# A two-layer hybrid encoder: the first loads in another order, the first two weight chunks by quarters, and GpSimd scaling part of the tokens

## What is computed

```python
def rmsnorm(x, g):
    y = x32 * lax.rsqrt(jnp.mean(x32 * x32, axis=-1, keepdims=True) + EPS)
    return (y * g).astype(x.dtype)

def hybrid_layer(x, c, ...):
    mod = jax.nn.silu(c) @ w_mod + b_mod
    shift, scale, gate = jnp.split(mod, 3, axis=-1)
    h = rmsnorm(x, norm_g) * (1.0 + scale[:, None]) + shift[:, None]
    z = h @ w_in          # 2752 columns, split among three groups of heads
    ...                   # convolution, latent attention, windowed attention
    out = jnp.concatenate([out_conv, out_mla, out_swa], axis=-1) @ w_out
    return x + gate[:, None] * out, states
```

## Time and profile before

| what | value |
|---|---|
| runs | 1207.41, 1207.62, 1209.09 us; median 1207.62 |
| the profiled execution: its own time | 1207.39 us |
| its span, first to last instruction | 1205.6 us, so 1.8 us lie around it |
| TensorE (PE) busy | 96% of the span |
| VectorE (DVE), ScalarE (ACT), GpSimd (POOL) busy | 52%, 36%, 5% |
| TensorE begins with chunk 0 | 41.79 us |
| TensorE begins with chunk 2 | 73.31 us |

### The profile page before, as it was taken

The page is one execution under the profiler, slowest core; times in us unless marked ns, Lnnn a source line. Parts: engine busy times, 40 slices in busy tenths (PEclk is TensorE's granted clock), DMA queues, the critical chain, the costliest instruction groups (busy, mean ns, idle before and its releaser), DMA issues.

```text
span 1205.6 us, 17889 instructions
## 1 busy us (share of the span) xinstructions
PE 1159.5 (96%) x7246; PEld 1039.4 (86%) x7246; DVE 623.6 (52%) x1063; ACT 436.7 (36%) x768; POOL 57.9 (5%) x46
## 2 busy tenths in 40 slices
PE   4699999999999999999999999999999999999996
PEld 3589999999996666789999999999999766769996
DVE  4852333336458866663385233233554886666135
ACT  3442221222246543441265323123223744445122
POOL 1000001000000000002130000100000000000211
PEclk9899999999999999999999999999999999999998
DMA  9621120111123244364131211111102342116003
GB/s 332 244 71 38 35 70 16 41 55 42 55 84 139 99 150 149 105 249 145 47 115 36 74 35 35 51 36 36 57 13 101 110 161 79 45 35 227 1 27 132
DMA packets 71884, 107.72 MB, mean 89 GB/s; under 512 B 3960, under 2 KB 59392, under 8 KB 70528
## 3 DMA queue, kind: packets, MB, share of 16 engines
q1 hardware_dynamic: 71808, 106.68, 26.4%
HBM read 93.91 MB, written 11.70 MB: 88 GB/s over the span
## 4 chain that ended last, share of the span: by engine, by line
PE 86%; DVE 8%; ACT 3%; DMA 1%; issue 1%; SPq 0%; POOLq 0%; DVEq 0%; ACTq 0%
PE psum L900 56%; PE psum L1264 5%; PE psum L1317 5%; PE psum L1296 2%; ACT rot L1462 1%; PE psum L891 1%; PE psum L1254 1%; DVE w_lo L1908 1%; DVE h_lo L1800 1%; PE psum L1331 1%; PE psum L1217 1%; PE psum L1253 1%; PE psum L1313 1%; PE psum L1102 1%; PE psum L1271 1%; PE psum L1274 1%
## 5 line engine op out<-in xcount | busy, mean ns | idle before, releaser
L900 PE MATMUL psum<-h_hi,w_hi 128*128 128x384 f32 x1392 | 473.3, 340 | 14.3 <-DVE h_lo L1858 9.3
L900 PE MATMUL psum<-h_lo,w_hi 128*128 128x384 f32 x1392 | 466.0, 335 | 0.0
L900 PE MATMUL psum<-h_hi,w_lo 128*128 128x384 f32 x1392 | 466.0, 335 | 0.0
L900 PEld LDWEIGHTS psum<-h_hi,w_hi 128*128 128x128 f32 x1392 | 261.9, 188 | 21.1 <-DVE h_lo L1858 10.1
L900 PEld LDWEIGHTS psum<-h_hi,w_lo 128*128 128x128 f32 x1392 | 262.1, 188 | 0.5 <-issue 0.5
L900 PEld LDWEIGHTS psum<-h_lo,w_hi 128*128 128x128 f32 x1392 | 261.9, 188 | 0.0
L1908 DVE TENSOR_TENSOR w_lo<-raw,w_hi 128x1024 fp32r<-128x1024 f32 x61 | 77.3, 1267 | 203.6 <-ACT w_hi L1457 202.9
L1457 ACT ACTIVATE w_hi<-raw 128x1024 fp32r<-128x1024 f32 (+1 forms) x62 | 65.3, 1053 | 252.7 <-PE psum L900 173.8
L1317 PE MATMUL psum<-pT,ckv 128*128 128x512 f32 x144 | 74.0, 599 | 1.6 <-DVE pT L1911 1.2
L1522 ACT ACTIVATE probs_p<-psum,nmax 128x128 f32<-128x128 f32 (+1 forms) x72 | 25.1, 361 | 120.8 <-DVE esink L1908 120.8
L1909 DVE SCALAR_TENSOR_TENSOR x<-psum,mod,x 128x768 f32<-128x768 f32 (+1 forms) x32 | 24.0, 751 | 67.4 <-PE psum L900 66.7
(11 more groups left out here) (240 smaller groups left out, 1457.6 us busy)
## 6 DMA issues: line engine op xcount, KB each, us to landing
raw<-in_w_in SPq DMA_DIRECT2D x18, 1024.0 KB, 5.4
raw<-in_w_mod SPq DMA_DIRECT2D x15, 1024.0 KB, 5.3
modw<-in_w_mod SPq DMA_DIRECT2D x8, 1024.0 KB, 13.7
raw<-in_w_out SPq DMA_DIRECT2D x10, 768.0 KB, 5.4
tab<-in_c_rope SPq DMA_DIRECT2D x6, 1152.0 KB, 5.3
x<-in_xT SPq DMA_DIRECT2D x3, 1536.0 KB, 9.3
x<-in_xT SPq DMA_DIRECT2D x2, 2304.0 KB, 10.9
x<-x_scratch SPq DMA_DIRECT2D x2, 2304.0 KB, 10.5
```

What stands on the lines that cost most here:

```text
L900: mm = pe.matmul(psum[:, bank, 0:BLK], w_[:, k, :], h[:, k, blk(n)], start=(k == 0 and i == 0), stop=(k == KD - 1 and i == 2))
```

## The change

SP issues the first loads in another order: block 0, the modulation's first quarter (two loads of 1 MiB from an array laid out for it), the first weights, blocks 1 and 2, then the three other quarters and the second weights. The modulation is made in four quarters with matmuls of 128 columns instead of 256. The products of chunks 0 and 1 are made by block and quarter (two groups `k`), in the order `FIRST`. ScalarE copies the spread means from PSUM to SBUF (`r_all`), so that GpSimd can read them too. GpSimd makes four of the six scalings of 128x1536, VectorE two. The orders on TensorE, VectorE and ScalarE are written anew. The core of the diff:

```diff
+FIRST = [(0, 0), (0, 1), (1, 0), (1, 1), (0, 2), (1, 2), (2, 0), (2, 1), (2, 2), (0, 3), (1, 3), (2, 3)]
+FIRST_VECTOR_SCALES = ((0, 0), (1, 0))
+FIRST_POOL_SCALES = ((0, 1), (1, 1), (2, 0), (2, 1))
...
+            load_first(0)
+            load_pair(0, 0, 0)
             for n in range(1, NBLK):
                 sp.dma_start(x[:, :, blk(n)], io["xT"][:, :, blk(n)]).then_inc(s_x[n].sem, 16)
...
+            for q in range(1, 4):
+                load_first(q)
+            load_pair(0, 1, 1)
...
+            def first_pool_scale(n, half):
+
+                pool.wait_ge(s_rc.sem, n + 1)
+                xs = x[:, 4 * half:4 * half + 4, blk(n)]
+                pool.tensor_tensor(xs, xs, r_all[:, blk(n)].unsqueeze(1).broadcast_to([P, 4, BLK]), ALU.mult)\
+                    .then_inc(s_xp.sem, 1)
+
+            first_root(0)
+            first_pool_scale(0, 1)
+            first_root(1)
+            first_root(2)
+            for n, half in FIRST_POOL_SCALES[1:]:
+                first_pool_scale(n, half)
...
+                    first_sums(0)
+                    first_row(0)
+                    first_spread(0)
+                    first_turn(0)
+                    first_sums(1)
+                    quarter(0, 0)
+                    first_spread(1)
+                    first_sums(2)
+                    first_row(1)
+                    first_turn(1)
+                    first_spread(2)
+                    quarter(0, 1)
+                    quarter(1, 0)
+                    first_row(2)
+                    quarter(1, 1)
+                    first_turn(2)
+                    quarter(0, 2)
+                    quarter(1, 2)
+                    first_row(3)
+                    quarter(2, 0)
+                    first_turn(3)
+                    quarter(2, 1)
+                    quarter(2, 2)
...
+                    quarter(2, 3).then_inc(z_done.sem, 1)
                     for n in range(NBLK):
+                        mm = key_products(n, range(6, 8))
...
+            def first_roots(n):
+
+                act.wait_ge(s_bc.sem, n + 1)
+                act.activation(r_all[:, blk(n)], psum[:, 3 + n, 0:BLK], ACT.Copy).then_inc(s_rc.sem, 1)
...
+            first_squares(1)
+            first_modulate(before, 0, 0)
+            first_squares(2)
+            first_roots(1)
+            first_roots(2)
+            for n, q in FIRST[1:]:
+                first_modulate(before, n, q)
...
             first_add(0)
             first_mean(0)
+            modulation_row(0)
             first_scale(0, 0)
             first_modulation(before, 0)
             first_modulate(0, 0)
+            w_rests(0)
             w_rests(1)
             first_lo(0, 0)
+            first_add(1)
+            first_mean(1)
+            first_add(2)
             modulation_row(1)
...
```

More of the change, by code:

```diff
@@ L269, in build @@
     w_uqr = at("w_uqr", RAW_AT + 8192, [P, 2, 2 * P])
-    modrow0 = at("modrow0", H_AT + 34816, [P, 2, 256])
+    modrow0 = [at(f"modrow0{i}", H_AT + 35840 + 512 * i, [P, P]) for i in range(2)]
     modrow = at("modrow", H_AT + 72704, [P, 256])
@@ L355, in build @@
     psum = nc.alloc_psum_tensor("psum", [P, 8, 512], F32)
-    modw = [[at(f"modw{half}{i}", H_AT + 18432 * half + 36864 * i, [P, 4, 2, 512]) for i in range(2)] for half in range(2)]
+    modw = [[at(f"modw{q}{i}", H_AT + 9216 * q + 36864 * i, [P, 4, 2, 256]) for i in range(2)] for q in range(4)]
     x_kept = nc.dram_tensor("x_scratch", (P, KD, NTOK), F32).ap()
@@ L453, in build @@
     s_x = [sg(f"tokens_landed{n}") for n in range(NBLK)]
-    s_modw = [[sg(f"first_modulation_landed{half}{i}") for i in range(2)] for half in range(2)]
+    s_modw = [[sg(f"first_modulation_landed{q}{i}") for i in range(2)] for q in range(4)]
     s_masks = sg("masks_landed")
@@ L778, in layer, with first_root @@
                 add_squares(lane, sq_b, KD)
-            for n in range(NBLK):
+            def first_root(n):
                 pool.wait_ge(s_mean.sem, n + 1)
@@ L841, in first_spread, with first_row, first_turn @@
                 for i in range(3):
-                    mm = pe.matmul(psum[:, (1, 2, 5)[n], tile(i)], rstd[:, 3 * n + i:3 * n + i + 1].broadcast_to([P, P]), ident[:],
+                    mm = pe.matmul(psum[:, 3 + n, tile(i)], rstd[:, 3 * n + i:3 * n + i + 1].broadcast_to([P, P]), ident[:],
                                    start=True, stop=True)
                 mm.then_inc(s_bc.sem, 1)
[L846 to L864, removed]
+            def first_row(q):
+                if q:
+                    pe.wait_ge(s_rowc.sem, q)
+                for part in range(2):
+                    pe.wait_ge(s_modw[q][part].sem, 16)
+                    for k in range(4):
+                        for i in range(4):
+                            mm = pe.matmul(psum[32 * i:32 * i + 32, 6, 0:P], cT[:, 4 * part + k, :],
+                                           modw[q][part][:, k, i // 2, tile(i % 2)],
+                                           start=(part == k == 0), stop=(part == 1 and k == 3))
+                mm.then_inc(s_row.sem, 1)
+            def first_turn(q):
+                pe.wait_ge(s_rowc.sem, q + 1)
+                if q:
+                    pe.wait_ge(s_modc.sem, q)
+                pe.matmul(psum[:, 7, 0:4 * (1 + NB)].rearrange("p (i c) -> p i c", i=4), modrow0[q % 2][:], strips,
+                          start=True, stop=True).then_inc(s_mod.sem, 1)
             pe.wait_ge(s_const.sem, 16)
@@ L1392, in _, with first_squares @@
             act.activation(csil[:], craw[:], ACT.Tanh, scale=0.5).then_inc(s_cs.sem, 1)
-            for n in range(NBLK):
+            def first_squares(n):
                 act.wait_ge(s_x[n].sem, 16)
@@ L1848, in first_modulate @@
                     before.link(dve.tensor_tensor(xs, xs, each(mod[:, 0, ks, 1:]), ALU.add))
-                for k in (4 * half, 4 * half + 1):
-                    ins = dve.tensor_scalar(x[:, k, cols], x[:, k, cols], amul[:, k, 0:1], mod[:, 0, k, 0:1],
-                                            ALU.mult, ALU.add)
-                before.link(ins, s_h)
-            def first_lo(n, half):
-                ks = slice(4 * half, 4 * half + 4)
-                dve.wait_ge(hi_h.sem, NBLK * half + n + 1)
+                before.link(dve.tensor_scalar(x[:, k, cols], x[:, k, cols], amul[:, k, 0:1], mod[:, 0, k, 0:1],
+                                              ALU.mult, ALU.add), s_h)
```

169 lines of the change are left out of this document (80 added, 89 removed).

## The result

The changed kernel takes 1237.62 us (median of 4 runs, 1236.71 to 1238.40) against 1207.74 of the original measured beside it: ratio 1.0241, 95% interval 1.0227 to 1.0256, slower by 29.9 us. The forecast was 1233.6 in 1218.5 to 1243.5, slower with a chance of 0.93.

The account below looks back on a forecast made before the run. The prediction took TensorE, busy 96% of the span, as the bound, with chunk 0's end carrying through: 1207.4 us profiled plus 26.2 us later made 1233.6 us, range 1218.5 to 1243.5.

Parts of the forecast that it names:

- What bounds: TensorE, busy 96% of the span: any shift of chunk 0's end, 69.31 us before, goes through to the end in full.
- the first product: TensorE's first product of chunk 0 was to start at 37.6 us, 4.2 us earlier than before.
- Loads cost nothing: Modulation quarters, 5.5 us of DMA each, land before they are needed, with cover of 3 us and 6 to 33 us.
- The row of a quarter: TensorE's 32 matmuls of 128 columns per modulation quarter: 2.2 us at the high clock, 3.8 at the low.
- GpSimd and VectorE exclude each other: VectorE instructions with two SBUF operands wait up to 3.3 us each while GpSimd scales; four meetings.
- the walk: Step-by-step timing of the new start: chunk 0 ends at 95.5 us against 69.31, 26.2 us more.
- rival (b): Milder slowdown of +7 to +18 us, from the high clock all through or no exclusion between the engines; chance 0.22.
- no exclusion: GpSimd and VectorE not locking each other out in the new start would take 8 us off; no separate chance.
- The low clock: After idling 8.6 us from 47.1, TensorE is at the low level, where a quarter's products take 3.3 us, not 1.75.
- the high level all through: TensorE keeping its 2.4 GHz clock throughout the new start would take 9 us off; no separate chance.
- The written order: In chunk 0's queues VectorE waits for rows queued behind products, then TensorE for `h_lo`; idle gaps sum to 20.4 us.
- Rival (c): Faster: TensorE fed without gaps from 37.6 us, so chunk 0 ends at 67.1, 2.2 us early; chance 0.04.

Follow-up runs that it names:

- experiment 1: Changed kernel with its four GpSimd scalings given back to VectorE, GpSimd making only the powers: 1226.97 us, ratio 1.0153 to the original.
- experiment 5: Changed kernel with VectorE's two scalings reading the spread roots from PSUM instead of ScalarE's SBUF copy: 1232.13 us, ratio 1.0203 to the original.
- 6: Original with GpSimd making four scalings from ScalarE's copies and VectorE's other two reading the copy too: 1215.55 us, ratio 1.0056.
- experiment 7: Original with the modulation's first quarter and first weights loaded ahead of blocks 1 and 2: 1217.12 us, ratio 1.0067.
- Experiment 9: Start rewritten with the changed kernel's loads and quarters; scalings on VectorE from PSUM, early rows, turns and adds, more ScalarE modulation, four-group sums: 1200.04 us, ratio 0.9928 to original.
- 10: Kernel of Experiment 9 with one of six scalings, (2, 1), given to GpSimd from a ScalarE copy: 1203.84 us, ratio 0.9957 to the original.
- 11: Kernel of Experiment 9 with modulation shared between VectorE and ScalarE as in the changed kernel: 1205.30 us, ratio 0.9975 to the original.
- experiment 2: Changed kernel with rows 2 and 3, their turns and VectorE copies moved earlier, GpSimd's scalings kept: 1224.31 us, ratio 1.0134 to the original.
- experiment 3: Changed kernel with all scalings on VectorE and also rows 2 and 3 early: 1219.07 us, ratio 1.0088 to the original.
- experiment 4: Changed kernel with matmuls nobody reads put ahead of six long TensorE waits in chunk 0: 1233.73 us, ratio 1.0207 to the original.
- experiment 8: Changed kernel with blocks 1 and 2 loaded ahead of the first quarter and first weights, as in the original: 1241.38 us, ratio 1.0269.

## Why the prediction was right, step by step

**What bounds.** Right. One moment, the end of chunk 0, carried nearly everything: +27.5 in the profile against +26.2. The shift went through all later stages, except for 1.6 us that the prediction did not have: the 600 products behind chunk 2's start. In thirteen traces they take either about 104.25 us (the original and experiments 1, 5, 6, 7, 9, 10 and 11) or 105.8 (the changed kernel and 2, 3, 4 and 8), the latter with a low clock in their first microseconds (0.53 from 103.5 to 105.5 us above). From the end of chunk 0 to these products it is 4.0 us in all thirteen, and TensorE is idle for 1.9 of them in ten traces (1.2 in the original, 6 and 7); of these ten, five kept the high level and five lost it. What decides stays open. The prediction came out 4.0 us low in all: 1.3 at the end of chunk 0, these 1.6, 0.9 by which the profiled execution was faster than the median, and small pieces. The 1.3 is in part luck: the first product came 1.4 us early and the second quarter 2.2 late.

**Loads cost nothing.** Right for this kernel: no engine waits for a modulation quarter, and experiment 8 shows that the new load order even gains 3.8 us. Experiment 7 shows that this holds only with the new queues.

**The row of a quarter.** 1.93 us high and 3.21 (partly low) against 2.2 and 3.8, mis-sized by 0.3 and 0.6. That row 0 began low is read from durations: the profile's clock column says 1.00 ahead of 23 us, but the sums just before took 2.72 us there, as long as the next ones did at 0.50 (33.47), where the third took 1.23 at the high level. The estimate of 1.8 us that the prediction worked out by the rule of the Trainium skill (TensorEngine Tiling (Array Packing), section Instruction Overhead), half of the row of 256 columns, was closer at the high level; the trace agrees within 0.13.

**The first product** came at 36.19, not 37.6: 0.6 from row 0, 0.6 from a spread at the high level, the rest handovers.

**GpSimd and VectorE exclude each other.** Right, with sizes of 4.87 and 4.07 us for the scaling and `h_lo` that the walk had at 5.1 and 4.3. Missed: the tensor_scalar (`x L1903`) is locked out as well, 3.66 us. The walk had counted only instructions with two SBUF operands, so product (0, 1) came at 57.9 instead of 55.7. Of the two parts of rival (b), "no exclusion" was put at 8 us. No run has GpSimd scale without excluding anything; the nearest are experiment 1 (no scaling on GpSimd, 7 us more work for VectorE), 10.3 us, and experiment 5 (part of the exclusion lifted), 4.2 us of chunk 0.

**The low clock.** The mechanism was there, its price was not. The prediction gave 9 us to "the high level all through"; experiment 4 had it from the second quarter on and gained 3.4 there. What it left low ahead of 41 us, row 0 and the first quarter, would by an estimate from the rows add 2.8 (3.21 less 1.93, and 1.5 of ten products): about 6, not 9. From 83 us on VectorE was next to wait for.

**The written order.** The walk had rows 2 and 3 and their copies in each other's way, and experiment 2 prices that at 12.8 us, the clock's share in that stretch included. Rival (c), TensorE fed without gaps once started, put chunk 0's end at 67.1 and was given 0.04 for this order. Experiment 9 did just that with another order, later still at the first product, and reached 62.05.

**The account** of 27.5 us: alone, 10.3 are GpSimd's scalings and 12.8 the late rows, 19.3 both together. The other 8.2 are not split by a run of their own, but the windows say where they lie. Between first product and end of chunk 0 TensorE is busy for 24.96 us and idle for 2.56 in the original, 37.24 and 23.35 in the changed kernel, 34.03 and 8.59 in experiment 3. So the 27.5 are 20.8 more of idling and 12.3 more of work, less the 5.6 by which it starts earlier; in experiment 3 the 8.2 are 6.0 and 9.1, less 6.9. The added work is sums, spreads and rows that now stand behind the first product instead of ahead of it, and more products at the low clock. The early first product had bought little by itself. Experiment 9 puts most of the small work ahead again and has 21.65 and 0.01. The clock's part, 3 to 6 us, lies across all of these.

## What to carry to other kernels

Work given to GpSimd to relieve VectorE has to be priced as exclusive time unless VectorE's instruction is of a kind seen to run beside it (here: one operand from PSUM): here 3.4 us on GpSimd replaced 1.76 on VectorE and stopped it for 2.9 to 3.2 us at each meeting. Where two engines feed each other in turn, put the producer of the next hand-over (row, copy, turn) ahead of the bulk work in both queues, and judge an order by the gaps behind the first product, not by how early it starts. Before pricing a faster resource, walk the chain once more without it and see who is last then.

## What the runs showed of the hardware

- A VectorE tensor_scalar of 384 elements with one SBUF tensor and per-partition scalars, 0.48 us alone, took 3.66 when it met a GpSimd scaling. So did `amul` of 18 elements (3.08 against 0.19). In the changed kernel the four locked-out instructions, of 18 to 1536 elements, waited 2.9 to 3.2 us each, whatever their width. Why a tensor_scalar with one SBUF tensor is excluded is not shown. The original's trace has it at half the time for each further element (420 ns for 384, 753 for 1024) that a tensor_tensor needs (691 ns for 512, 1226 for 1024).
- The exclusion goes both ways: GpSimd's power of 3 elements took 2.30 instead of 0.85 us when it met VectorE's add of 1536.
- Reading one operand from PSUM lifts it for a tensor_tensor: 1.75 us against 4.87 at the same place, while GpSimd was scaling.
- 58 products of 384 columns that nobody reads kept the granted clock at 1.00 through the 10 us up to 56.5, where the changed kernel had 0.50 from 50 to 56 us. A wait of 4.3 us without them (29.5 to 33.75) was followed by 0.50 from 34.5 to 41 us.
